# A mixture-of-experts decoder layer on one core: first expert weights in two 4 MB transfers instead of four 2 MB transfers

## The reference, cut to what matters

```python
logits = xt @ router_w + router_b
top_val, top_idx = lax.top_k(logits, 4); gates = softmax(top_val)
# for every expert e and the rows xb routed to it:
gu = xb @ w_gu[e] + b_gu[e]                  # w_gu[e]: 1024 x 2048
x_glu = minimum(gu[:, :1024], 7.0)
x_lin = clip(gu[:, 1024:], -7.0, 7.0)
act = x_glu * sigmoid(1.702 * x_glu) * (x_lin + 1.0)
y = act @ w_down[e] + b_down[e]              # w_down[e]: 1024 x 1024
# y is weighted by its gate and added to its token's row
```

## Time and profile before

| | |
|---|---|
| Median of three runs | 1240.03 us |
| The profiled execution's own time | 1242.82 us |
| Its span (first to last instruction) | 1241.0 us |
| PE busy (matmul) | 1128.7 us, 91% |
| VectorE, ScalarE, GpSimd busy | 342.2, 220.3, 223.0 us |
| DMA | 54238 packets, 450.01 MB, mean 363 GB/s |
| Chain that ended last | DMA 43%, PE 39%, issue 7% |
| `gu` loads | 128 DMAs of 2048 KB, 28.0 us to landing (median) |
| `dn` loads | 64 DMAs of 2048 KB, 23.3 us to landing (median) |

### The profile page before, as it was taken

One profiled execution on the slowest core, in us unless ns is written; L12 is line 12 of the kernel. 1 busy time (PEld: TensorE's weight loads), 2 busy tenths in 40 slices (PEclk: granted clock), 3 DMA queues, 4 the chain that ended last, 5 costly groups with the idle time before them and its releaser, 6 DMA issues.

```text
span 1241.0 us, 17621 instructions
## 1 busy us (share of the span) xinstructions
PE 1128.7 (91%) x7410; PEld 584.3 (47%) x7410; DVE 342.2 (28%) x595; ACT 220.3 (18%) x361; POOL 223.0 (18%) x99
## 2 busy tenths in 40 slices
PE   7969879999999998898989999999999998988985
PEld 7859779999433333333333333343333333333332
DVE  5982686332411122111111111131111111111112
ACT  5336735634200000000000000000000000000001
POOL 5938966685000000000000000000000000000000
PEclk8989989999999999999999999999999999999998
DMA  8434426669899999999999989999999999999993
GB/s 247 177 135 144 145 86 253 236 209 418 368 421 427 428 428 429 429 428 428 429 428 428 429 361 430 429 427 429 428 429 428 429 429 427 430 428 428 428 428 167
DMA packets 54238, 450.01 MB, mean 363 GB/s; under 512 B 7136, under 2 KB 9248, under 8 KB 29472
## 3 DMA queue, kind: packets, MB, share of 16 engines
q1 hardware_dynamic: 54064, 449.06, 87.6%
q0 software_dynamic: 144, 0.52, 0.1%
HBM read 448.00 MB, written 1.05 MB: 362 GB/s over the span
## 4 chain that ended last, share of the span: by engine, by line
DMA 43%; PE 39%; issue 7%; POOL 5%; DVE 3%; ACT 1%; SPq 1%; POOLq 0%; DVEq 0%
DMA gu<-in_w_gu 23%; DMA dn<-in_w_down 20%; PE ps L684 12%; PE ps L649 11%; POOL w_lo L373 5%; PE ps L625 3%; PE ps L426 2%; PE ps L422 2%; PE ps L423 2%; PE ps L592 2%; PE ps L672 1%; ACT w_hi L739 1%; SPq L261 1%; PE ps L446 1%; PE ps L441 1%
## 5 line engine op out<-in xcount | busy, mean ns | idle before, releaser
L649 PE MATMUL ps<-gu,xg 128*64 128x512 f32 x2048 | 453.5, 594 | 39.0 <-DMA gu<-in_w_gu 39.0
L649 PEld LDWEIGHTS ps<-gu,xg 128*64 128x64 f32 x2048 | 143.2, 137 | 331.2 <-issue 251.6
L684 PE MATMUL ps<-dn,actT 128*64 128x512 f32 x1024 | 234.9, 611 | 26.9 <-DMA dn<-in_w_down 26.7
L373 POOL TENSOR_TENSOR w_lo<-land,w_hi 128x1024 fp32r<-128x1024 f32 x80 | 217.8, 2748 | 76.0 <-ACT w_hi L739 75.9
L1195 DVE TENSOR_SCALAR g<-ps 128x512 f32<-128x512 f32 x32 | 22.1, 692 | 730.4 <-PE ps L649 730.4
L684 PEld LDWEIGHTS ps<-dn,actT 128*64 128x64 f32 x1024 | 71.7, 140 | 186.5 <-issue 143.2
L422 PE MATMUL ps<-x_hi,w_hi 128*128 128x256 f32 x384 | 98.0, 291 | 10.8 <-ACT w_hi L739 5.8
L887 ACT ACTIVATE wT<-ps 128x256 f32<-128x256 f32 x32 | 12.3, 384 | 488.8 <-PE ps L657 488.8
L423 PE MATMUL ps<-x_lo,w_hi 128*128 128x256 f32 x384 | 96.8, 288 | 0.0
L739 ACT ACTIVATE w_hi<-land 128x1024 fp32r<-128x1024 f32 x80 | 80.1, 1052 | 53.1 <-PE ps L426 39.4
L893 ACT ACTIVATE y_sb<-ps 128x512 f32<-128x512 f32 x32 | 19.1, 597 | 365.4 <-PE ps L684 365.4
(11 more groups left out here) (246 smaller groups left out, 889.9 us busy)
## 6 DMA issues: line engine op xcount, KB each, us to landing
gu<-in_w_gu SPq DMA_DIRECT2D x128, 2048.0 KB, 28.0
dn<-in_w_down SPq DMA_DIRECT2D x64, 2048.0 KB, 23.3
land<-in_w_in SPq DMA_DIRECT2D x13, 2048.0 KB, 8.1
land<-in_w_proj_rnn SPq DMA_DIRECT2D x2, 2048.0 KB, 8.8
land<-in_w_proj_attn SPq DMA_DIRECT2D x2, 2048.0 KB, 8.8
land<-in_w_out SPq DMA_DIRECT2D x2, 2048.0 KB, 7.7
land<-in_w_in SPq DMA_DIRECT2D x2, 1024.0 KB, 10.3
x_sb<-in_x SPq DMA_DIRECT2D x2, 512.0 KB, 3.9
```

The costliest lines, as they stand in the source:

```text
L373: pool.tensor_tensor(w_lo[:, q % PIECES], land[q // PIECES][:, :, (q % PIECES) * P:(q % PIECES + 1) * P], w_hi[:, q % PIECES].bitcast(f32) ...
L649: last = mm(ps[64 * h:64 * h + 64, 4 + c, :], xg[:, k * SLOTS:(k + 1) * SLOTS], gu[par][m][:, r, c * D + h * HALF:c * D + (h + 1) * HALF], ...
L684: last = mm(ps[64 * h:64 * h + 64, 6, :], actT[:, j, half * SLOTS:(half + 1) * SLOTS], dn[half][:, j, h * HALF:(h + 1) * HALF], start=half ...
```

## The change

`GU_RUN` goes from 2 to 4: an expert's gu lies in two tiles of 32 KB per partition, and from expert 2 on it comes as two DMAs of 4 MB whose 128 runs are 32 KB long. Each of the two is issued when both chunks that its tile takes the place of have been used (`wait(2 * m + 1)`). PE still works in four chunks and still counts `gu_used` four times per expert, but waits for data only before chunks 0 and 2. Experts 0 and 1, whose space comes free piece by piece, keep their four 2 MB transfers under semaphores of their own (`load_early`), at the same places of SP's order.

```diff
-GU_RUN = 2
+GU_RUN = 4
-        gu = [[at(f"gu{par}_{m}", 96 * par + 16 * m, [P, GU_RUN, 2 * D]) for m in range(4)] for par in range(2)]
+        gu = [[at(f"gu{par}_{m}", 96 * par + 32 * m, [P, GU_RUN, 2 * D]) for m in range(2)] for par in range(2)]
-        gu_landed = [[sem(f"gu_landed{p}_{m}") for m in range(4)] for p in range(2)]
+        gu_landed = [[sem(f"gu_landed{p}_{m}") for m in range(2)] for p in range(2)]
+        early_landed = [[sem(f"early_landed{p}_{m}") for m in range(4)] for p in range(2)]
+            def load_early(par, m):
+                src = w_gu_rows[par * D:(par + 1) * D, :].rearrange("(p k) n -> p k n", p=P)
+                sp.dma_start(gu[par][m // 2][:, m % 2 * 2:m % 2 * 2 + 2, :], src[:, 2 * m:2 * m + 2, :]).then_inc(
+                    early_landed[par][m], 16)
-            def load_gu(row, par, wait, ms=range(4)):
+            def load_gu(row, par, wait):
                 src = w_gu_rows[ds(row, D), :].rearrange("(p k) n -> p k n", p=P)
-                for m in ms:
-                    wait(m)
+                for m in range(2):
+                    wait(2 * m + 1)
                     sp.dma_start(gu[par][m][:, :, :], src[:, GU_RUN * m:GU_RUN * m + GU_RUN, :]).then_inc(
                         gu_landed[par][m], 16)
...
-            load_gu(0, 0, lambda m: sp.wait_ge(lo_ready, 76 + 4 * m), [0, 1])
-            load_gu(0, 0, lambda m: sp.wait_ge(filled, 40), [2, 3])
+            for m in range(2):
+                sp.wait_ge(lo_ready, 76 + 4 * m)
+                load_early(0, m)
+            sp.wait_ge(filled, 40)
+            load_early(0, 2)
+            load_early(0, 3)
...
                 for m in range(4):
-                    pe.wait_ge(gu_landed[par][m], 8 * E + 16)
+                    if early:
+                        pe.wait_ge(early_landed[par][m], 16)
+                    elif m % 2 == 0:
+                        pe.wait_ge(gu_landed[par][m // 2], 8 * E)
...
-                    for r in range(GU_RUN):
-                        k = GU_RUN * m + r
+                    for r in range(2):
+                        k = 2 * m + r
...
-                                          gu[par][m][:, r, c * D + h * HALF:c * D + (h + 1) * HALF],
+                                          gu[par][m // 2][:, m % 2 * 2 + r, c * D + h * HALF:c * D + (h + 1) * HALF],
```

More of the change, by code:

```diff
@@ L309, in _ @@
                 if u == 15:
-                    load_gu(D, 1, lambda m: sp.wait_ge(s_filled, H), [0])
+                    sp.wait_ge(s_filled, H)
+                    load_early(1, 0)
                 if u == 16:
-                    load_gu(D, 1, lambda m: sp.wait_ge(filled, 28), [1])
+                    sp.wait_ge(filled, 28)
+                    load_early(1, 1)
             load_dn(0, lambda h: sp.wait_ge(filled, 36), [0])
-            load_gu(D, 1, lambda m: sp.wait_ge(filled, 36), [2])
-            load_gu(D, 1, lambda m: sp.wait_ge(mix_ready, 4), [3])
-            load_gu(0, 0, lambda m: sp.wait_ge(lo_ready, 76 + 4 * m), [0, 1])
-            load_gu(0, 0, lambda m: sp.wait_ge(filled, 40), [2, 3])
+            sp.wait_ge(filled, 36)
+            load_early(1, 2)
+            sp.wait_ge(mix_ready, 4)
+            load_early(1, 3)
+            for m in range(2):
[4 more added lines that the diff above has]
+            load_early(0, 3)
             def load_pair(E, row):
@@ L626, in combine, with expert @@
                        y_sb[64 * h:64 * h + 64, :], start=False, stop=False)
-            def expert(E, X, par, meanwhile=None, first=False, at_once=False):
+            def expert(E, X, par, meanwhile=None, first=False, at_once=False, early=False):
                 if first:
@@ L691, in expert @@
                     combine(par, 1)
-            expert(0, 0, 0, lambda: (open_y(0), open_y(1)), first=True)
-            expert(0, 0, 1, add_b_down)
+            expert(0, 0, 0, lambda: (open_y(0), open_y(1)), first=True, early=True)
+            expert(0, 0, 1, add_b_down, early=True)
             with pe.Fori(1, N_E // 2, 1) as i:
```

## The result

The changed kernel takes 1242.03 us (median of 20 runs, 1240.21 to 1243.85), the kernel before 1239.99 (20 runs, 1238.69 to 1241.57). The ratio is 1.0017, 95% interval 1.0011 to 1.0024: 2.0 us slower, within 1.4 and 3.0. The forecast was +2.4 us, at the edge of what can be told from no change. The prediction gave slower (above 1242.5) 0.52 and no difference that can be told 0.40. The median lies 0.5 us on the side of the second; only the 20 runs of each kernel set it apart from zero.

What follows compares the result with a forecast made beforehand. The prediction took the stream of bytes, its holes and PE's work after the last gu landing to bound the time. Hole 3.42, end 3.43, packets -4.6 and clock +0.1 gave +2.4 us, 1242.4 us, range 1239.4 to 1247.0.

Steps and rivals of the forecast that it cites:

- What bounds the kernel: Whole kernel: the stream of bytes sets the time, 29.37 us per expert after the turn against PE's 25.75.
- The hole: Start of the stream, 320 us: expert 2's first 4 MB waits for both chunks, costing 3.42 us, paid in full.
- No further holes: Later gu loads: issued 3.4 us later but harmless, since at least 4.5 us of queue remain, at gu(3).
- What a transfer costs: Each 4 MB transfer of experts 2 to 31: half the packets save 0.076 us, 4.6 us over sixty.
- the rival of cut runs: Inside the queue: each 32 KB run is cut in two, saving under 0.4 us; 1246.6 us, chance 0.16.
- that of a further gain: Each 4 MB transfer after expert 2: stream gains more than packets say, up to 0.152 us each; 1237.9 us, chance 0.09.
- The end: After gu(31)'s last landing: PE has two chunks left in place of one, adding 3.43 us.
- The PE clock: Lower clock at the end costs 1.7 us (chance 0.75); changed phase at the turn returns 1.6 (0.6); both, +0.1.
- The sum: Whole kernel: 3.42 + 3.43 - 4.6 + 0.1 = +2.4 us, so 1240.03 becomes 1242.4.

Runs made afterwards that it cites:

- the repaired kernels: Changed kernel with expert 2's first 4 MB split into two 2 MB pieces: 1240.85 us with copied PE code, 1240.38 without; 1237.68 with expert 31's second 4 MB also split.
- two kernels: Changed kernel with 16 KB runs in its 4 MB transfers, 1247.58 us; kernel before with 2 MB transfers issued and awaited in pairs from expert 2, 1247.82 us.
- the kernel with the copy alone: Changed kernel with experts 30 and 31 copied out of PE's loop and nothing else: 1242.45 us, 1.0022 of the kernel before.
- the best version: Changed kernel with expert 2's first 4 MB split without copied code and expert 31's second 4 MB split with a copy: 1237.68 us, 0.9984 of the kernel before.

## Why the prediction was right

- *What bounds the kernel.* Right. Every edit to the stream's pace moved the time by pace times count, within its interval, and PE, which does the same work, followed.
- *The hole.* Its mechanism and size hold on the kernel before: 3.1 us measured for 3.42. Taking it out of the changed kernel gave 2.0 and not 3.4, still within the interval. In the traces the repaired kernels have lost 1.2 to 2.4 us of the 3.4 again by the landing of gu(3)'s first 4 MB.
- *No further holes.* Right for the changed kernel, where no landing from 360 us to the turn is more than 0.25 us off its beat. The prediction counted on the grown hole to keep the queue long enough at gu(3). That margin is thin: without the hole, landings there come late.
- *What a transfer costs.* Right, and the best founded term: 0.077 us saved per 4 MB for 0.076, packets to the last but one. Both the rival of cut runs (1246.6) and that of a further gain (1237.9) fall with it. The former is at the same time the price of the grain alone, which two kernels show at 1247.6 and 1247.8. The fixed 2.0 us that the prediction quotes from the Trainium skill ("DMA: Bandwidth & Descriptors", Anatomy of one DMA) are that page's fit for transfers issued by GpSimd, and SP issues these. Here halving the number of transfers at the same runs changed the pace by less than 0.01 us each (9.787 for 2 x 4.895), so in a full queue nothing of a fixed cost was left to save.
- *The end.* Right: +3.05 us between the executions, and 2.6 to 2.9 as a repair against a kernel with the same copy, of which the first 4 MB of expert 31 hides half a microsecond, for 3.43.
- *The PE clock.* Here the number came out by luck. The two parts were to cancel, 1.7 at the end against 1.6 at the turn, and neither came as described. At the end I had given 0.75 to the lower clock. In the profiled execution, PE does fall to the lower level (1.2 GHz) after most waits of 2.62 us, but a slow pass of 8.6 us makes it late for the next piece, so it then waits for 1.78 only and stays at 2.4 GHz. In this trace slow and fast passes alternate but for one place, and the last expert was spared. I left out that one slow pass shortens the next wait. It doesn't always protect: with 4 MB of 16 KB runs, 8.78 us followed a wait of 2.02 right after a slow pass, and the last expert there was hit after 2.70. At the turn the higher clock came, as was taken as likely (3.74 us for 5.44), but it brought 0.8 us and not 1.6, since the second half of dn(14) then had to be waited for.
- *The sum.* Medians: 3.1 + 3.1 - 4.6 = +1.6 by the measured parts, or some +1.1 without the copy that the second holds, each part known to about 1.2 us; +2.4 forecast, +2.0 measured.

## What to carry to other kernels

Where a queue of transfers is never empty, a longer run saves only the fixed time of each packet, here 8.7 ns per run, so 1.4% of the pace of 16 KB runs is all that is left, and half of it is had by doubling. The larger grain costs at the two ends of the stream, where a buffer comes free piece by piece and where PE works off the last piece; keep fine pieces there and long runs between. The two costs and their repairs aren't independent of the rest: a hole that is closed lets the next weak place of the queue show, and a piece that is split only helps until the whole piece ahead of it is what PE waits for. A change worth 0.2% can come out the other way round in a single pair of profiles: compare pieces of the traces with the medians of many runs beside them.

## What the runs showed of the hardware

- Instruction fetches of 16 KB run on the same DMA engines as the weights. A landing near one came 1.08 us late in the kernel before, 0.23 in the changed kernel at the same place, and 0.86 in the kernel with the copy alone. Unrolling two experts of PE's program brought two more of them into the launch (24 for 22).
- Two 2 MB transfers and one of 4 MB take the same time to 0.01 us if the runs are the same (9.79). The length of the run sets the pace: 4.895 us per 2 MB with 16 KB runs, 0.072 more with 8 KB, 0.039 less with 32 KB.
- A run of 32 KB travels as one packet (45597 packets in all, 45598 if none is cut).
- After waits of 2.6 to 2.7 us PE mostly ran the next 32 gu matmuls in 8.5 to 8.8 us (six of seven times in the changed kernel), after 1.8 us or less in 7.09. Waits of 1.94 to 2.1 us went either way: 8.78 us after 1.94 at the turn of the best version, 7.09 after 2.06 at 827.45 in the changed kernel.
